# Both halves of the first two units projected without the norm, in the head of a gated conv layer on one core

## The reference

```python
hn = rms_norm(h, norm_g[layer])          # x * rsqrt(mean(x*x) + eps) * g
z = hn @ w_in                            # 1024 x 3072
a, b, gate = jnp.split(z, 3, axis=-1)
u = a * jax.nn.sigmoid(b)
u = depthwise causal conv of u, 31 taps, + conv_b
uf = layer norm of u over channels, * ln_g + ln_b
u = jax.nn.silu(uf) * jax.nn.silu(gate)
return h + u @ w_out
```

## Time and profile before

| what | value |
| --- | --- |
| time before, median of 3 runs | 408.78 us (408.66 to 409.11) |
| the profiled execution's own time | 410.54 us |
| its span in the trace | 408.7 us |
| PE busy | 385.2 us, 94% |
| DVE busy | 330.3 us, 81% |
| ACT busy | 203.8 us, 50% |
| POOL busy | 251.3 us, 61% |

### The profile page before, as it was taken

One profiled execution on the slowest core, in us unless ns is written; L12 is line 12 of the kernel. 1 busy time (PEld: TensorE's weight loads), 2 busy tenths in 40 slices (PEclk: granted clock), 3 DMA queues, 4 the chain that ended last, 5 costly groups with the idle time before them and its releaser, 6 DMA issues.

```text
span 408.7 us, 4697 instructions
## 1 busy us (share of the span) xinstructions
PE 385.2 (94%) x1704; PEld 308.7 (76%) x1704; DVE 330.3 (81%) x392; ACT 203.8 (50%) x259; POOL 251.3 (61%) x146
## 2 busy tenths in 40 slices
PE   3989999999999999999999989999886969999997
PEld 2768888888888888888888878888665747888886
DVE  5588999889999999999999999999878855560111
ACT  6677453535094476485666656463762531640000
POOL 0526549949479999999998999988275440000000
PEclk9999999999999999999999999999996998999999
DMA  8982111200310111102112011110113260057111
GB/s 294 404 349 68 51 40 51 103 2 0 103 54 0 51 53 52 53 0 63 42 57 97 2 51 51 55 32 20 53 52 103 64 245 0 2 165 297 54 51 51
DMA packets 12119, 34.06 MB, mean 83 GB/s; under 512 B 1344, under 2 KB 1856, under 8 KB 12096
## 3 DMA queue, kind: packets, MB, share of 16 engines
q1 hardware_dynamic: 11808, 33.56, 23.1%
q10 hardware_dynamic: 288, 0.21, 0.2%
HBM read 29.57 MB, written 4.19 MB: 83 GB/s over the span
## 4 chain that ended last, share of the span: by engine, by line
PE 43%; DVE 38%; issue 7%; POOL 6%; ACT 3%; DMA 1%; SPq 1%; POOLq 0%; DVEq 0%; ACTq 0%
DVE acc L826 29%; PE mm L372 20%; PE acc L444 12%; PE mm L444 8%; POOL pconv L1052 5%; PE mm L438 2%; DMA raw<-w_in 1%; DVE u L778 1%; DVE dconv L802 1%; DVE x_lo L869 1%; POOL wo_lo L1014 1%; DVE acc L817 1%; DVE stats L834 1%; DVE sgate L862 1%; PE mm L427 1%
## 5 line engine op out<-in xcount | busy, mean ns | idle before, releaser
L826 DVE SCALAR_TENSOR_TENSOR acc<-u,chan,acc 128x1024 f32<-128x1024 f32 (+1 forms) x194 | 197.2, 1092 | 1.5
L1052 POOL TENSOR_TENSOR pconv<-pconv,prod 128x512 f32<-128x512 f32 (+1 forms) x83 | 154.2, 1857 | 17.9 <-ACT prod L575 9.0
L372 PE MATMUL mm<-x_hi,w_hi 128*128 128x512 f32 x384 | 155.3, 404 | 9.9 <-DVE x_lo L734 7.7
L372 PE MATMUL mm<-x_lo,w_hi 128*128 128x512 f32 x384 | 153.2, 399 | 0.0
L372 PE MATMUL mm<-x_hi,w_lo 128*128 128x512 f32 x384 | 153.1, 399 | 0.0
L575 ACT ACTIVATE prod<-u,chan 128x512 f32<-128x512 f32 (+1 forms) x93 | 85.0, 937 | 71.0 <-POOL pconv L1052 54.5
L372 PEld LDWEIGHTS mm<-x_hi,w_hi 128*128 128x128 f32 x384 | 72.9, 190 | 29.2 <-issue 8.5
L372 PEld LDWEIGHTS mm<-x_hi,w_lo 128*128 128x128 f32 x384 | 73.0, 190 | 17.8
L372 PEld LDWEIGHTS mm<-x_lo,w_hi 128*128 128x128 f32 x384 | 73.1, 190 | 16.6
L1005 POOL TENSOR_TENSOR w_lo<-raw,w_hi 128x1024 fp32r<-128x1024 f32 x23 | 55.5, 2413 | 27.3 <-ACT w_hi L546 27.3
L444 PE MATMUL acc<-wo_hi,x_hi 128*128 128x512 f32 (+1 forms) x80 | 33.3, 416 | 9.4 <-DVE x_lo L869 5.2
(11 more groups left out here) (65 smaller groups left out, 336.5 us busy)
## 6 DMA issues: line engine op xcount, KB each, us to landing
raw<-w_in SPq DMA_DIRECT2D x23, 512.0 KB, 3.3
nat<-x_t SPq DMA_DIRECT2D x16, 256.0 KB, 8.2
sgate<-x SPq DMA_DIRECT2D x8, 512.0 KB, 10.4
raw<-w_out SPq DMA_DIRECT2D x8, 512.0 KB, 3.2
nat<-x SPq DMA_DIRECT2D x8, 512.0 KB, 5.6
y<-nat SPq DMA_DIRECT2D x15, 256.0 KB, 7.7
raw<-w_in SPq DMA_DIRECT2D x2, 256.0 KB, 3.8
y<-nat SPq DMA_DIRECT2D x2, 128.0 KB, 1.8
```

Of the source, the lines that this page charges most:

```text
L372: ins = nc.tensor.matmul(bank(("unit", m, h)), w[:, m % 3, k, :], xx[:, k, half(h)], start=(k == 0 and i == 0), stop=(k == KC - 1 and i == 2))
L826: ins = nc.vector.scalar_tensor_tensor(dst, u_in(j, halves, k), w, running, ALU.mult, ALU.add)
L1052: nc.gpsimd.tensor_tensor(dst, prod[:, (p - 1) % 3, width] if k == 1 else dst, prod[:, p % 3, width], ALU.add).then_inc(sums_done, 1)
```

## The change

Half 0 of units 0 and 1 is now projected without the norm too, and half 1 is the first whose norm is made. The passes of the head become (0,1), (1,1), (0,0), (1,0), (2,1), (3,1), (2,0), (3,0); `project_pair` is gone. The rows of tiles 4 to 7 are loaded, squared and inverted first, between the columns of half 0, and those of tiles 0 to 3 come after the third weight tile. `spread_rms(1)` stands inside pass (0,0), before k = 6; `spread_rms(0)` stands at the start of pass (3,1). The inverse of tiles 0 to 3 is one POOL instruction pair instead of four. POOL makes the low parts of k = 1, 3 of half 1 and k = 1, 3, 5, 7 of half 0. The tables for the time after the head are as they were.

```diff
-LAG = 1
-LO_BY_POOL = ((), (0, 1, 5))
+LO_BY_POOL = ((1, 3, 5, 7), (1, 3))
-DIAG_AT = {2: [4], 3: [5, 6], 4: [7]}
-ROWS_AT, SQUARE_AT = (2, 3, 4, 5), (-1, 1, 2, 3)
-SPREAD_AT = (6, 5)
+ROW_ORDER = (4, 5, 6, 7, 0, 1, 2, 3)
+ROWS_BEFORE = {0: (4, 5), 2: (6,), 4: (7,)}
+DIAG1_AFTER = {1: (4, 5), 3: (6,), 7: (7,)}
+DIAG0_AFTER = {7: (0, 1, 2, 3)}
+SPREAD_AT = {(0, 0, 6): 1, (3, 1, 0): 0}
...
-        PASSES = [(0, 1), (1, 1), (0, 0), (1, 0), (2, 0), (3, 0), (2, 1), (3, 1)]
+        PASSES = [(m, h) for pair in (0, 2) for h in (1, 0) for m in (pair, pair + 1)]
...
@@ SP
-            for t in range(TPH):
-                load_rows(t)
-            for k in range(KC):
-                load_columns(0, k)
-                if k in ROWS_AT:
-                    load_rows(TPH + ROWS_AT.index(k))
-            sp.wait_ge(w0lo_ready, 2)
-            load_weights(2)
-            for m in range(3, NU):
+            for k in range(KC):
+                for t in ROWS_BEFORE.get(k, ()):
+                    load_rows(t)
+                load_columns(0, k)
+            sp.wait_ge(w0lo_ready, 2)
+            load_weights(2)
+            for t in range(TPH):
+                load_rows(t)
+                if t == 1:
+                    sp.wait_ge(wlo_ready, 1)
+                    load_weights(3)
+            for m in range(4, NU):
...
@@ ACT
-            for t in range(TPH):
-                square(t)
-            for k in range(-1, KC):
-                if k >= 0:
-                    split_x(0, k)
-                if k in SQUARE_AT:
-                    square(TPH + SQUARE_AT.index(k))
+            for k in range(KC):
+                for t in ROWS_BEFORE.get(k, ()):
+                    square(t)
+                split_raw(0, k)
             split_w(2)
-            sigmoid_scaled()
-            split_w(3)
-            read_unit(0, 0)
             for k in range(KC):
                 split_x(1, k)
+                if k == 6:
+                    sigmoid_scaled(1)
+                if k in (1, 3, 5, 6):
+                    square((1, 3, 5, 6).index(k))
+                if k == 5:
+                    split_w(3)
+            for k in range(KC):
+                split_x(0, k)
+                if k == 3:
+                    sigmoid_scaled(0)
...
@@ DVE
             for k in range(1, KC):
-                split_raw(k)
-            copy_gate()
-            for t in range(TPH):
-                rms_diagonal(t)
+                split_raw(1, k)
+            for k in range(KC):
+                split_raw(0, k)
+                if k == 0:
+                    copy_gate(1)
+                for t in DIAG1_AFTER.get(k, ()):
+                    rms_diagonal(t)
+            make_hn(1, 0)
+            scale_gate(1)
+            for k in range(KC):
+                if k + 1 < KC:
+                    make_hn(1, k + 1)
+                if not by_pool(1, k):
+                    split_x(1, k)
+                if k == 1:
+                    copy_gate(0)
+                if k == 6:
+                    conv_in_raw(1)
+                for t in DIAG0_AFTER.get(k, ()):
+                    rms_diagonal(t)
             make_hn(0, 0)
+            scale_gate(0)
             for k in range(KC):
                 if k + 1 < KC:
                     make_hn(0, k + 1)
                 if not by_pool(0, k):
                     split_x(0, k)
-                for t in DIAG_AT.get(k, []):
-                    rms_diagonal(t)
-            scale_gate()
-            for k in range(KC):
-                make_hn(1, k)
-                if k == 3:
-                    conv_in_raw()
-                if k > 0 and not by_pool(1, k - 1):
-                    split_x(1, k - 1)
-                if k == 5:
-                    conv_in(1, 0)
-            if not by_pool(1, KC - 1):
-                split_x(1, KC - 1)
+                if k == 4:
+                    conv_in_raw(0)
...
@@ POOL
-            for t in range(NT):
-                inverse_rms(t)
+            for t in ROW_ORDER[:TPH]:
+                inverse_rms([t])
             finish_w_lo(2)
+            for k in LO_BY_POOL[1]:
+                finish_x_lo(1, k)
             finish_w_lo(3)
-            for k in range(KC):
-                if by_pool(1, k):
-                    finish_x_lo(1, k)
+            inverse_rms(range(TPH))
+            for k in LO_BY_POOL[0]:
+                finish_x_lo(0, k)
```

More of the change, by code:

```diff
@@ L256, in arrival, with half_order, raw_order, hn_order @@
         def arrival(j, h):
-            return NH * j + h + 1 if j else NH - h
+            return NH * j + 1 + (h if j > 1 else 1 - h)
+        def half_order(m):
+            return (1, 0) if m < 4 else (0, 1)
+        def raw_order(h, k):
+            return KC * (1 - h) + k
+        def hn_order(h, k):
+            return KC * (1 - h) + k
+        def row_order(t):
+            return ROW_ORDER.index(t)
         def nth(kind, m):
@@ L291, in wait_lo, with rms_spread @@
         def wait_lo(engine, h, k):
-            before = [(hh, kk) for hh in range(NH) for kk in range(KC) if (hh, kk) <= (h, k)]
+            earlier = [(hh, kk) for hh in range(NH) for kk in range(KC) if hn_order(hh, kk) <= hn_order(h, k)]
             mine = by_pool(h, k)
-            engine.wait_ge(xlo_pool if mine else xlo_ready, sum(by_pool(*hk) == mine for hk in before))
+            engine.wait_ge(xlo_pool if mine else xlo_ready, sum(by_pool(*hk) == mine for hk in earlier))
+        def rms_spread(h):
+            return acc[:, h, :]
         block = ctx.enter_context(nc.Block())
@@ L364, in spread_rms @@
                 for i in range(TPH):
[L365 to L366 removed]
+                    pe.wait_ge(diag_ready, row_order(TPH * h + i) + 1)
+                    ins = nc.tensor.matmul(rms_spread(h)[:, i * P:(i + 1) * P], ones[:], diag(h, i), start=True, stop=True)
                 ins.then_inc(rms_all_ready, 1)
@@ L382, in project_raw @@
                     if m == 0:
-                        if k == 0:
+                        if (h, k) == (1, 0):
                             pe.wait_ge(w0lo_ready, 1)
-                        if k == KC // 2:
+                        if (h, k) == (1, KC // 2):
                             pe.wait_ge(w0lo_ready, 2)
[L387 to L402, removed]
+                        pe.wait_ge(xlo_raw, raw_order(h, k) + 1)
+                    if (m, h, k) in SPREAD_AT:
+                        spread_rms(SPREAD_AT[m, h, k])
+                    unit_terms(m, h, k)
             def project(m, h):
@@ L449, in _ @@
             pe.wait_ge(ones_ready, 1)
-            for m in range(2):
-                project_raw(m)
-            project_pair()
+            for m, h in PASSES[:4]:
+                project_raw(m, h)
             for m, h in PASSES[4:]:
@@ L513, in square, with split_raw @@
                                      accum_out=mean_sq[:, t:t + 1]).then_inc(sumsq_ready, 1)
-            def split_raw(k):
-                act.wait_ge(xt_in[1][k], 16)
-                nc.scalar.activation(x_hi[:, k, half(1)], nat[:, k, half(1)], ACT.Copy,
+            def split_raw(h, k):
+                act.wait_ge(xt_in[h][k], 16)
+                nc.scalar.activation(x_hi[:, k, half(h)], nat[:, k, half(h)], ACT.Copy,
                                      scale=norm_g[:, k:k + 1]).then_inc(xhi_raw, 1)
@@ L920, in _ @@
                 if UNITS[m][0] == "a":
-                    conv_in(m, 0)
+                    conv_in(m, half_order(m)[0])
                 while done < min(STEPS_BY[m][2], last_step):
@@ L984, in inverse_deviation, with inverse_rms @@
                                         ALU.pow).then_inc(rstd_ready, 1)
-            def inverse_rms(t):
-                part = slice(t, t + 1)
-                pool.wait_ge(sumsq_ready, t + 1)
+            def inverse_rms(tiles):
+                part, done = slice(tiles[0], tiles[-1] + 1), row_order(tiles[-1]) + 1
+                pool.wait_ge(sumsq_ready, done)
                 nc.gpsimd.tensor_scalar(mean_sq[:, part], mean_sq[:, part], 1.0 / D, RMS_EPS, ALU.mult,
-                                        ALU.add).then_inc(ms_ready, 1)
-                pool.wait_ge(ms_ready, t + 1)
+                                        ALU.add).then_inc(ms_ready, len(tiles))
+                pool.wait_ge(ms_ready, done)
                 nc.gpsimd.tensor_tensor(rms[:, part], mean_sq[:, part], half_neg[:, part],
-                                        ALU.pow).then_inc(rms_ready, 1)
+                                        ALU.pow).then_inc(rms_ready, len(tiles))
             def finish_x_lo(h, k):
-                pool.wait_ge(xhi_ready, KC * h + k + 1)
+                pool.wait_ge(xhi_ready, hn_order(h, k) + 1)
                 nc.gpsimd.tensor_tensor(x_lo[:, k, half(h)], nat[:, k, half(h)], x_hi[:, k, half(h)].bitcast(F32),
```

76 lines of the change are left out of this document (38 added, 38 removed).

## The result

| | before | after |
| --- | --- | --- |
| median of the paired runs | 408.94 us (408.66 to 410.63, 4 runs) | 418.79 us (415.2 to 419.28, 4 runs) |
| profiled execution: own time, span | 410.54, 408.7 | 419.0, 417.2 |
| steps of DVE begin | 46.64 | 55.77 |
| DVE adds POOL's sum (the join) | 83.75 | 92.14 |
| first aggregate of the layer norm | 283.28 | 291.96 |

The change made the kernel slower by 2.2%: the ratio is 1.0222, with a 95% interval of 1.019 to 1.0254. The forecast was 413.2 us with a range up to 415.3, so the direction was right and the size too small by 5.6 us. A second set of six executions (first experiment) gave 416.78 us, so the miss is 3.6 to 5.6 us.

What follows compares the result with a forecast made beforehand. The prediction took PE and DVE as full together from 83.7 to 286 us; DVE's head 7.7 us later, less 3.26 us reserve, gave a 4.4 us shift, from 408.78 to 413.2 us, range 409.4 to 415.3.

Steps and rivals of the forecast that it cites:

- Two engines are full together: From 83.7 to 286 us PE and DVE are both almost always busy, so DVE's lateness at 84 us reaches the end.
- d: How much later DVE's head ends and its convolution steps begin than in the kernel before; forecast 7.7 us.
- The reserve of 3.26 us: DVE's wait for POOL's sum of tile 0 ahead of the join, 80.49 to 83.75 us, taken to absorb lateness.
- p: How much later PE ends the half of unit 2 that POOL's sum follows; forecast 3.0 us.
- The split against POOL's `w_lo`: In half 1, DVE's low part of k = 6 collides with POOL's instruction and ends 0.57 us after it, at 39.7.
- The floor: Rival: ACT and POOL fit between DVE's instructions without a stall; shift 1.0 us, 409.8 to 411.5 us; chance 0.2.
- the faster rival: PE's 2.1 us gain in the head comes through, with DVE's steps beginning before 49.9; 407.7 us; chance 0.12.
- POOL's sum is there at 86.8: At the join, POOL's sum is ready before DVE arrives at 88.2, so DVE waits under 0.5 us or not at all.
- the exchange of halves after the head: The switch of the order of halves behind the head, costed at nothing.
- The 29.9 us: Fixed distance from PE's end of unit 2's half to the join, used to place POOL's sum.
- the larger of d - 3.26 and p: Rule for how much later everything behind the join comes; forecast 7.7 - 3.26 = 4.4 us.
- The clock: Rival: PE's new stalls at 38 to 42 us lower the granted clock, adding 4.6 us to p; 416.4 us; chance 0.06.

Runs made afterwards that it cites:

- run 1: The changed kernel executed again in a second set, no edit (also called the first experiment): 416.78 us, ratio 1.0193.
- run 7: The kernel before, with 3 more taps on DVE ahead of its convolution steps, results unused: 410.57 us, ratio 1.0035.
- run 8: The kernel before, with 9 more taps on DVE ahead of its convolution steps, results unused: 415.99 us, ratio 1.0165.
- run 2: The changed kernel with DVE making the fourth `u` after 9 convolution steps instead of 17: 413.82 us, ratio 1.0115.
- run 6: The changed kernel with the edits of run 2, run 4 and run 5 together: 412.55 us, ratio 1.008.
- run 10: The changed kernel with the join of tile 0 three steps later in DVE's list: 413.64 us, ratio 1.0107.
- run 3: The kernel before, with ACT's sigmoid of unit 4, half 0, made to wait for the fourth `u`: 408.99 us, ratio 0.9993.
- run 4: The changed kernel with the first spread before k = 4 instead of k = 6, tile 7's diagonal after the sixth raw split: 414.57 us, ratio 1.0145.
- run 5: The changed kernel with half 1's sigmoid and fourth square behind ACT's last high part, second spread before k = 7 of (2,1): 415.56 us, ratio 1.0151.
- run 11: The kernel of run 6 with all rows of half 1 first and the first spread at the head of (0,0): 412.15 us, ratio 1.0072.

## Why the prediction was right and where it failed

**Right.** Two engines are full together behind the join, and lateness of DVE beyond a reserve reaches the end: runs 7 and 8 show it at d = 4.55 and 9.51. The reserve of 3.26 us on DVE's own path was read rightly: where the join has no wait, it is later by d less 3.2 (4.47 at 7.63 in run 2, 2.74 at 5.91 in run 6). The order of events in the head, with each instant within 0.5 us in run 1, whose clock was full there: first `make_hn` 27.40 (27.2), k = 6 done 39.68 (39.7), PE's waits 1.12 and 1.27 (1.55 and 1.5, a little too large), second `make_hn` 43.87 (43.9), steps 54.18 (54.3). PE's part too: ACT's sigmoid of (2,0) stands at 56.89, 3.03 us behind the 53.86 of the kernel before, where p = 3.0 was forecast. The split against POOL's `w_lo` took 2.46 us, as in the earlier trace rows: the second occurrence of it, and the price that was taken. The floor (shift 1.0) and the faster rival are out: d was 7.5.

**The failed step.** "POOL's sum is there at 86.8", and with it the cost of nothing for "the exchange of halves after the head". The 29.9 us from the end of (2,0) to the sum were taken from the old order, where ACT never waits for DVE on the way (the earlier trace rows shows only its first wait). In run 1 they are 33.6 (56.89 to 90.53). In the new order the sum hangs on the fourth `u`, and that is made by DVE, 21 us and 17 steps behind its late start (55.77 to 76.85). So the sum is not later by PE's p but follows DVE's d, and "the larger of d - 3.26 and p" lacks a term: by run 1 the join is later by d less 0.76, and even in the old order, by runs 7 and 8, by d less 2.5. Run 2 (that `u` moved) and run 10 (the join moved) each take 3.0 to 3.1 us off the median of run 1, and 2.3 and 2.4 off the time of its first aggregate. Run 3 shows that this wait is free without lateness, run 8 that lateness with the old halves leaves 0.77 of it. The two together are the cause: of 2.5 us some 0.8 come with lateness in the old order too (at d = 4.55 as at 9.51), and some 1.75 from the crossing of the halves, which puts a sigmoid and a product ahead of the second sigmoid. The forecast said what the join should show (a wait under 0.5 us), but put no case of a longer one among the rivals.

**The size that a rival had.** The clock was given 0.06, at a price of 4.6 us on PE. It came in parts of the executions and smaller. In the first profile the second stall was followed by matmuls 0.43 us apart, which made the second spread end and so DVE's head 1.6 us later (45.47 against 43.87). In the profiles of runs 1, 4, 5 and 8 the fall comes behind the stall of 3.3 to 3.4 us that ends between 98 and 100 us. The argument against it (the first stall of the old head had left the clock at 1.00) rested on two waits of 0.82 and 0.30 us, and here two waits of 1.12 and 1.27 us follow one another within 2.3 us.

**The sum.** First profile: join at 92.14 against a forecast of 88.2. 2.55 us of it are the wait for POOL, 1.4 the later head (d = 9.13 against 7.7), which is the clock's work there. Span 417.2 against 413.1, the same 4.1. The median of run 1 lies 3.6 us above the forecast: 3.0 of it went with run 2, which takes the crossing away and with it most of PE's stall near 98 us (0.94 of 3.34 is left). In the two profiles 2.3 of the 3.0 are there at the first aggregate, and they are the join: from the join to the aggregate it is 199.8 us in both, though in run 1 the granted clock is 0.82 from 101.5 to 110 us and in run 2 it is 1.00. It is 199.8 in the first profile as well, and 201.0 in run 4, where the clock fell further. The remaining 0.7 of the 3.0 lie in executions that were not profiled, and their cause stays open. The last 0.6 of the 3.6 us are those of run 2 itself: 0.3 by which its first aggregate is later than its join, and 0.3 that the medians can't tell.

**What stays open.** Why the granted clock falls in one execution and not in another of the same kernel. And what sets the end of half 1 in run 11, where only one possible cause was named.

## What to carry to other kernels

When halves or tiles are reordered, go through every wait whose count is worked out from that order, and ask which instruction writes the item it now counts up to, and when; a wait that costs nothing in the old order can be the longest of the kernel when its writer is late. Work out the time at a join for each engine that feeds it by its own chain, through all engines in it, and not by a fixed distance from an older trace. Work added for one engine in the head must be paid at the engine that has least in reserve there: PE was ahead after the raw passes and DVE was 7.5 us late.

## What the runs showed of the hardware

**The clock behind short stalls.** In the executions profiled here, stretches at less than full clock stand behind waits of PE, but not behind each of them: after 1.12 and 1.27 us of waiting at 39 to 42 us the matmuls were 0.43 us apart in one execution and 0.24 in another, and after 3.4 us of waiting near 98 us the clock was 0.50 in run 4 for 3.5 us and 1.00 in the first profile.

**The part between the aggregates.** From the first to the second aggregate it takes 45.5 to 48.3 us whatever the head did, and goes by the clock granted there, over the same work. First the changed kernel's first profile, then that of run 1:

```profile
292.00:340.00 48.00, 41.28 (x182) 32.17 (x181) 38.21 (x54) 24.70 (x34) 22.31 (x13) 0.93 0.28 95
```

```profile
290.40:336.10 45.70, 38.91 (x182) 30.36 (x181) 37.47 (x54) 24.75 (x34) 23.11 (x13) 1.00 0.28 100
```

So 2.4 us of the 4.6 between these two executions come from there, and have nothing to do with the change. This was in the kernel before too, and whoever compares two single profiles of these kernels has to take it out first.

**One input tile does not keep DVE clear of POOL.** The taps added in runs 7 and 8 have one tile as input (the other is a scalar per partition) and write `dconv`, in SBUF. Eight of the nine in run 8 took 0.75 us. In run 7 the second one met a `w_lo` of POOL:

```profile
47.59 2.71 DVE L914 TENSOR_SCALAR dconv<-u,chan 128x1024 f32<-128x1024 f32 x1
```

```profile
47.12 2.62 POOL L1013 TENSOR_TENSOR w_lo<-raw,w_hi 128x1024 fp32r<-128x1024 f32 x1 [2.69 <-ACT w_hi L547]
```

It ended at 50.30, 0.56 us behind POOL, as the splits with two input tiles do. The same operation on the same tile with its result in `acc`, which is in PSUM, takes 1.28 us and lost nothing beside that `w_lo`: two of them take 2.47 us here, where POOL works, and in run 7 from 51.19 us, where POOL is idle. This is the kernel before:

```profile
47.83 1.28 DVE L817 TENSOR_SCALAR acc<-u,chan 128x1024 f32<-128x1024 f32 x1
```

```profile
47.03 2.41 POOL L1005 TENSOR_TENSOR w_lo<-raw,w_hi 128x1024 fp32r<-128x1024 f32 x1 [2.69 <-ACT w_hi L546]
```

So whoever writes to SBUF there pays up to 2 us for one tap. What decides between the two, the place of the result or the faster pace, was not tried by itself.
